# One encoder layer with product-key experts: alternating sum banks, later exponentials, eight diagonals, and an earlier load of the first merged rows

## The reference, cut to what matters

```python
h = rmsnorm(x)                        # per row
z = h @ w_in                          # attention, convolution, memory queries, gates
merged = g0 * attention(z) + g1 * conformer_conv(z) + g2 * memory_attention(z)
x = x + merged @ w_out
h = rmsnorm(x)
q = (h @ w_q).reshape(rows, 8, 2, 128)              # 8 heads, two halves each
s1, s2 = q[:, :, 0] @ keys1.T, q[:, :, 1] @ keys2.T # 128 side scores each
v1, i1 = top_k(s1, 16);  v2, i2 = top_k(s2, 16)
top, pos = top_k(v1[:, None] + v2[None, :], 16)     # 16 of 256 sums
idx = (i1 * 128 + i2)[pos]                          # one of 16384 experts
g = softmax(top)
act = gelu((h * u[idx]).sum(-1))                    # a row of u for each expert
x = x + (g * act * v[idx]).sum(experts)             # a row of v for each expert
```

## Time and profile before

| what | us |
|---|---|
| median of 3 runs | 3762.02 (3761.2 to 3765.11) |
| the profiled execution | 3731.85 |
| its span in the trace | 3730.0 |
| TensorE (PE) busy | 3340.5 (90%) |
| VectorE busy | 2929.1 (79%) |
| GpSimd busy | 2148.8 (58%) |
| ScalarE busy | 1418.8 (38%) |
| the chain that ended last: PE, VectorE, DMA, issue, POOL | 50%, 13%, 9%, 5%, 5% |

### The profile page before, as it was taken

The page is one execution under the profiler, slowest core; times in us unless marked ns, Lnnn a source line. Parts: engine busy times, 40 slices in busy tenths (PEclk is TensorE's granted clock), DMA queues, the critical chain, the costliest instruction groups (busy, mean ns, idle before and its releaser), DMA issues.

```text
span 3730.0 us, 44666 instructions
## 1 busy us (share of the span) xinstructions
PE 3340.5 (90%) x13326; PEld 2204.9 (59%) x13326; DVE 2929.1 (79%) x6686; ACT 1418.8 (38%) x2932; POOL 2148.8 (58%) x1831
## 2 busy tenths in 40 slices
PE   8999899899999949898799999999977898888966
PEld 7787555444444436666688887888844364453722
DVE  5499763467988958999988898888877878788865
ACT  5235674122442213333344444545433142332510
POOL 6221233155556545777766666676655666575776
PEclk9999999999999979999899999999988998999999
DMA  6415565698999979999999999999999999898999
GB/s 211 126 48 141 139 175 191 210 357 318 347 390 367 339 283 372 360 383 372 407 410 397 410 394 411 381 408 400 392 403 409 355 326 410 286 400 329 317 390 369
DMA packets 443310, 1224.37 MB, mean 328 GB/s; under 512 B 65250, under 2 KB 153478, under 8 KB 442047
## 3 DMA queue, kind: packets, MB, share of 16 engines
q0 software_dynamic: 239616, 872.52, 61.0%
q1 hardware_dynamic: 177162, 313.45, 24.1%
q10 hardware_dynamic: 26293, 35.54, 2.8%
HBM read 1129.03 MB, written 92.31 MB: 327 GB/s over the span
## 4 chain that ended last, share of the span: by engine, by line
PE 50%; DVE 13%; DMA 9%; issue 5%; POOL 5%; ACT 1%; SPq 0%; ACTq 0%; DVEq 0%; POOLq 0%
PE open_q_and_scores_ps L2807 18%; PE open_sums_ps L1916 8%; PE open_q_and_scores_ps L2864 4%; PE open_sums_ps L2890 4%; PE open_h_T_ps L1930 4%; DVE late_x L3290 4%; PE open_h_T_ps L2785 3%; DMA late_v_rows<-in_peer_v,table_twin_idx 3%; POOL late_v_rows L2666 2%; POOL late_u_rows L2666 2%; DVE late_u_rows L3267 2%; PE open_h_T_ps L2791 2%; PE open_h_T_ps L2717 1%; PE open_sums_ps L1856 1%; DMA open_weight_columns<-in_w_in 1%
## 5 line engine op out<-in xcount | busy, mean ns | idle before, releaser
L2666 POOL DMA_INDIRECT late_v_rows<-in_peer_v,late_kept_idx x573 | 584.4, 1020 | 210.0 <-issue 161.2
L2653 POOL DMA_INDIRECT late_u_rows<-in_peer_u,late_kept_idx x320 | 478.7, 1496 | 265.1 <-DVE late_dots L3267 205.3
L3267 DVE CUSTOM_DVE_ANT_0 late_u_rows<-late_u_rows,open_rows_ps 128x1024 f32<-128x1024 f32 x432 | 522.4, 1211 | 13.0 <-DMA late_u_rows<-in_peer_u,late_expert_idx 9.1
L3290 DVE SCALAR_TENSOR_TENSOR late_x<-late_v_rows,late_weights,late_x 128x1024 f32<-128x1024 f32 x368 | 471.5, 1281 | 10.0 <-DMA late_v_rows<-in_peer_v,late_expert_idx 6.7
L2807 PE MATMUL open_q_and_scores_ps<-table_h_T_upper,table_u_T_upper 128*128 128x512 f32 x1024 | 424.4, 414 | 0.0
L2807 PE MATMUL open_q_and_scores_ps<-table_h_T_lower,table_u_T_upper 128*128 128x512 f32 x1024 | 402.7, 393 | 0.0
L2807 PE MATMUL open_q_and_scores_ps<-table_h_T_upper,table_u_T_lower 128*128 128x512 f32 x1024 | 402.2, 393 | 0.0
L2890 PE MATMUL open_sums_ps<-late_v_rows,late_diag 128*128 128x512 f32 (+1 forms) x600 | 299.8, 636 | 85.3 <-DMA late_v_rows<-in_peer_v,late_kept_idx 34.3
L2666 POOL DMA_INDIRECT late_u_rows<-in_peer_v,late_kept_idx x259 | 284.1, 1097 | 147.2 <-issue 66.3
L2890 PE MATMUL open_sums_ps<-late_u_rows,late_diag 128*128 128x512 f32 x512 | 266.0, 660 | 84.5 <-DMA late_u_rows<-in_peer_v,late_kept_idx 43.2
L1829 POOL DMA_INDIRECT open_u_rows<-in_peer_u,late_expert_idx x115 | 161.0, 1400 | 256.5 <-DVE late_dots L2269 130.8
(11 more groups left out here) (466 smaller groups left out, 7599.2 us busy)
## 6 DMA issues: line engine op xcount, KB each, us to landing
table_u_block<-in_peer_u SPq DMA_DIRECT2D x128, 512.0 KB, 7.7
scr_scores<-table_scores SPq DMA_DIRECT2D x32, 1024.0 KB, 16.6
open_weight_columns<-in_w_in SPq DMA_DIRECT2D x64, 256.0 KB, 5.9
table_first_scores<-scr_scores SPq DMA_DIRECT2D x4, 4096.0 KB, 16.1
table_second_scores<-scr_scores SPq DMA_DIRECT2D x4, 4096.0 KB, 15.6
front_w_raw<-in_w_in SPq DMA_DIRECT2D x48, 256.0 KB, 5.0
scr_m<-open_gated SPq DMA_DIRECT2D x42, 256.0 KB, 6.1
late_v_rows<-in_peer_v,late_kept_idx POOLq DMA_INDIRECT x573, 8.8
```

The lines of the kernel that those rows point to most:

```text
L2653: pool.indirect_dma_start(u[k % U_RING][:], None, io["peer_u"][0], bass.IndirectOffsetOnAxis(ap=rows_of(n), axis=0)).then_inc(s_u[k % U_RI ...
L2666: pool.indirect_dma_start(slot[:], None, io["peer_v"][0], bass.IndirectOffsetOnAxis(ap=rows_of(m), axis=0)).then_inc(arrived, 16)
L3267: dve.tensor_tensor_reduce(u[k % U_RING][:], u[k % U_RING][:], h2_rows, 1.0, 0.0, ALU.mult, ALU.add, dots[:, n % COLS:n % COLS + 1]).then_ ...
L3290: dve.scalar_tensor_tensor(rows[:], slot[:], weight_of(m), rows[:], ALU.mult, ALU.add).then_inc(s_vsum, 1)
```

## The change

1. *Diagonals.* There are eight buffers instead of four; the four new ones lie in the table's part of SBUF.
2. *Exponentials and gates.* `exps` stands three steps behind piece 10, `gate` three steps behind piece 15 (`EXP_LAG`).
3. *Banks.* Tiles 4 and 6 sum in another pair of banks, `pRows`, tiles 3, 5 and 7 in `acc`. `keep_sum` and its semaphore are gone; `total` reads the banks. The first sum of tile 4 waits for the last dot product, that of a later tile t for `total` of tile t-2.
4. *First merged rows.* SyncE loads them behind `late_w_q_high` and ahead of the last two pairs of gated stores, into `late_h2_next` (which is in the place of a u buffer), once all units' products are done; the load after the last stores is gone. `turn_merged(1)` reads there, `normed(1)` waits until it has read, and the load of the h rows into `late_h2_next` waits for the same turn.
5. *Heads of tile 1.* The first four heads after that, R = 8 to 11, are heads 4 to 7 of the tile, which use `late_w_q_high`, and R = 12 to 15 are heads 0 to 3, so that `late_w_q_low` is waited for at R = 12 instead of 8.
6. *Residual of tile 1* stands two steps later on VectorE, as do its `square` and `normed`.

```diff
@@ -1328,3 +1328,4 @@
 COLS = 32
-DIAGS = 4
+DIAGS = 8
+EXP_LAG = 3
 HEADS_AHEAD, HEADS_KEPT = 4, 16
@@ -1348,2 +1349,4 @@
 GATE_AT = (0, 2, 1)
+HEAD_AT = [R - R % NH + (R + NH // 2) % NH if R // NH == 1 else R for R in range(HEADS)]
+HALF_FIRST = (FIRST_KEPT, NH + NH // 2)
 ROUTE, SCORES_READ = 23, 6
@@ -1497,2 +1500,3 @@
         self.row, self.ident = sb("row", [P, NK]), sb("identity", [P, P], BF16)
+        self.diag = [sb(f"diag{k}", [P, P]) for k in range(DIAGS // 2)]
         self.less_lane, self.one = sb("less_lane", [P, 1]), sb("one", [P, 1])
@@ -1765,2 +1769,9 @@
             load_chunk(j)
+        def load_first_merged(sp):
+            last = next(u for u in reversed(range(UNITS_OPEN)) if unit(u)[1] == 2)
+            sp.wait_ge(s_uprod, S0 + 2 * UNITS_OPEN)
+            for g in (2 * last, 2 * last + 1):
+                sp.wait_ge(s_mst[g % GATED_RING], S0 + 16 * (g // GATED_RING + 1))
+            sp.dma_start(L.h2_next[:], scr["m"][1]).then_inc(L.s_m, 16)
+
         for u in range(UNITS_OPEN):
@@ -1789,2 +1800,4 @@
                 load_conv(u + CONV_RING)
+            if u + 1 == UNITS_OPEN:
+                load_first_merged(sp)
             for h in range(2):
@@ -2416,3 +2429,3 @@
     ss, root, inv, twins, B = L.ss, L.root, L.inv, L.twins, L.table
-    dots, gl, wt, diag, qs, qT, u, v, tile_sum = L.dots, L.gl, L.wt, L.diag, L.qs, L.qT, L.u, L.v, L.tile_sum
+    dots, gl, wt, diag, qs, qT, u, v, tile_sum = L.dots, L.gl, L.wt, L.diag + L.table.diag, L.qs, L.qT, L.u, L.v, L.tile_sum
     top, topi, topf, hot = L.top, L.topi, L.topf, L.hot
@@ -2432,3 +2445,3 @@
     s_sq, s_root, s_inv = p.sem("x2_squares"), p.sem("x2_root"), p.sem("x2_scale")
-    s_x2, s_y, s_yout, s_tile = (p.sem(n) for n in ("x2_summed", "y_rows", "y_stored", "tile_sum"))
+    s_x2, s_y, s_yout = (p.sem(n) for n in ("x2_summed", "y_rows", "y_stored"))
     s_q, s_qk, s_qt, s_qtk, s_sc = (p.sem(n) for n in ("q", "q_kept", "q_turned", "qT_kept", "side_scores"))
@@ -2455,2 +2468,6 @@
 
+    def banks_of(t):
+
+        return pRows if t in TABLED[::2] else acc
+
     def two_back(R):
@@ -2512,8 +2529,4 @@
         def load_merged(t):
-            if t >= 2:
-                sp.wait_ge(s_hturn, S0 + t)
-                sp.wait_ge(s_h2out.sem, s_h2out.start + 16 * min(t - 1, SHORT))
-            else:
-                sp.wait_ge(s_hturn, S0 + 1)
-                sp.wait_ge(s_place, S0 + 1)
+            sp.wait_ge(s_hturn, S0 + t)
+            sp.wait_ge(s_h2out.sem, s_h2out.start + 16 * min(t - 1, SHORT))
             sp.dma_start(h2[:], scr["m"][NE if t == SHORT else prompt_tile(t)]).then_inc(s_m, 16)
@@ -2556,2 +2569,4 @@
                 sp.wait_ge(s_place, S0 + t)
+            else:
+                sp.wait_ge(s_mturn, S0 + 2)
             sp.dma_start(h2_next[:], scr["h2"][t]).then_inc(s_h2in.sem, 16)
@@ -2594,3 +2609,2 @@
 
-        load_merged(1)
         load_x_new(1)
@@ -2706,3 +2720,3 @@
             for k in range(KC):
-                src = h2[:, k * P:(k + 1) * P] if t else done.gated[k // 4][:, k % 4 * P:(k % 4 + 1) * P]
+                src = (h2_next if t == 1 else h2)[:, k * P:(k + 1) * P] if t else done.gated[k // 4][:, k % 4 * P:(k % 4 + 1) * P]
                 ins = pe.transpose(chain_banks(t)[:, k // 4, (k % 4) * P:(k % 4 + 1) * P], src, c.ident[:])
@@ -2731,5 +2745,6 @@
             else:
-                if R in (4, 8):
-                    L.w_q[R % NH // 4].wait(pe)
-                columns = L.w_q[R % NH // 4].buf[:, :, R % 4 * 2 * NK:(R % 4 + 1) * 2 * NK]
+                H = HEAD_AT[R]
+                if R in HALF_FIRST:
+                    L.w_q[H % NH // 4].wait(pe)
+                columns = L.w_q[H % NH // 4].buf[:, :, H % 4 * 2 * NK:(H % 4 + 1) * 2 * NK]
             pe.wait_ge(s_hT, S0 + R // NH + 1)
@@ -2753,3 +2768,3 @@
             for s in range(2):
-                ins = pe.matmul(pS[:, 0, s * NK:(s + 1) * NK], qT[:, s, :], keysT[:, 2 * (R % NH) + s, :], start=True, stop=True)
+                ins = pe.matmul(pS[:, 0, s * NK:(s + 1) * NK], qT[:, s, :], keysT[:, 2 * (HEAD_AT[R] % NH) + s, :], start=True, stop=True)
             ins.then_inc(s_sc, 1)
@@ -2879,5 +2894,5 @@
                 elif t == FIRST_TABLED:
-                    pe.wait_ge(s_y, S0 + 1)
-                elif t > FIRST_TABLED:
-                    pe.wait_ge(s_tile, S0 + t - FIRST_TABLED)
+                    pe.wait_ge(s_dot, S0 + DOTS[GATHER_END])
+                else:
+                    pe.wait_ge(s_y, S0 + t - FIRST_TABLED)
             if m == last_of(SHORT):
@@ -2889,3 +2904,3 @@
             for h in range(2):
-                ins = pe.matmul(acc[0:rows, h, :], diag[k % DIAGS][:, 0:rows], slot[:, h * BANK:(h + 1) * BANK],
+                ins = pe.matmul(banks_of(t)[0:rows, h, :], diag[k % DIAGS][:, 0:rows], slot[:, h * BANK:(h + 1) * BANK],
                                 start=(m == first_of(t)), stop=(m == last_of(t)), skip_group_check=True)
@@ -2957,7 +2972,7 @@
             act.wait_ge(s_sck.sem, s_sck.start + i + 1)
-            act.dma_start(scr["side"][R], L.side_stage[i % 2][:]).then_inc(s_scout[i % 2].sem, 16)
+            act.dma_start(scr["side"][HEAD_AT[R]], L.side_stage[i % 2][:]).then_inc(s_scout[i % 2].sem, 16)
 
         def load_side(R):
-            i = R - FIRST_KEPT
-            act.wait_ge(s_scout[i % 2].sem, s_scout[i % 2].start + 16 * (i // 2 + 1))
+            i, at = R - FIRST_KEPT, HEAD_AT.index(R) - FIRST_KEPT
+            act.wait_ge(s_scout[at % 2].sem, s_scout[at % 2].start + 16 * (at // 2 + 1))
             if i == 0:
@@ -2985,3 +3000,3 @@
                         keep_merged(t + 1)
-                    if t < NE and h == (2 if t == 0 else 6):
+                    if t < NE and h == (3 if t == 0 else 6):
                         square(t + 1)
@@ -3075,7 +3090,2 @@
 
-        def keep_sum(t):
-            act.wait_ge(s_sum, S0 + TENSOR_SUMS[tile_end(t)])
-            act.wait_ge(s_y, S0 + t - SHORT)
-            act.activation(tile_sum[:], acc[:].rearrange("p a n -> p (a n)"), ACT.Copy).then_inc(s_tile, 1)
-
         ahead = Names()
@@ -3107,8 +3117,5 @@
                 diagonal(m)
-            for R, piece in ROUTES_AT.get(n, ()):
+            for R, piece in ROUTES_AT.get(n - EXP_LAG, ()):
                 if piece == 10:
                     exps(R)
-            for t in TABLED[:-1]:
-                if n == tile_end(t) + TENSOR_LAG:
-                    keep_sum(t)
 
@@ -3237,2 +3244,4 @@
             dve.reciprocal(inv[:], root[:]).then_inc(s_inv, 1)
+            if t == 1:
+                dve.wait_ge(s_hturn, S0 + 1)
             dve.wait_ge(s_inv, S0 + t + 1)
@@ -3254,9 +3263,6 @@
             rows = SAM if t == SHORT else P
-            if t in (SHORT, NE):
-                dve.wait_ge(s_sum, S0 + TENSOR_SUMS[tile_end(t)])
-            else:
-                dve.wait_ge(s_tile, S0 + t - SHORT)
+            dve.wait_ge(s_sum, S0 + TENSOR_SUMS[tile_end(t)])
             dve.wait_ge(s_vsum, S0 + VECTOR_SUMS[tile_end(t)])
             dve.wait_ge(s_x2in[t % 2].sem, s_x2in[t % 2].start + 16 * ((t + 1) // 2))
-            rows_sum = acc[0:rows, :, :].rearrange("p a n -> p (a n)") if t in (SHORT, NE) else tile_sum[:]
+            rows_sum = banks_of(t)[0:rows, :, :].rearrange("p a n -> p (a n)")
             dve.tensor_tensor(summed(t)[0:rows, :], rows_sum, summed(t)[0:rows, :], ALU.add).then_inc(s_y, 1)
@@ -3307,5 +3313,5 @@
                 for h in range(NH - FIRST_KEPT if t == 0 else NH):
-                    if t < NE and h == (1 if t == 0 else 5):
+                    if t < NE and h == (2 if t == 0 else 5):
                         residual(t + 1)
-                    elif t < NE and h == (2 if t == 0 else 6):
+                    elif t < NE and h == (3 if t == 0 else 6):
                         normed(t + 1)
@@ -3365,3 +3371,3 @@
                 gate(2)
-            for R, piece in ROUTES_AT.get(n - 1, ()):
+            for R, piece in ROUTES_AT.get(n - EXP_LAG, ()):
                 if piece == TOPK - 1:
```

2 lines of the change are left out of this document (1 added, 1 removed).

## The result

The changed kernel takes 3734.94 us (median of 4 runs, 3730.49 to 3739.79), the kernel before 3761.61 (3759.85 to 3765.11, 4 runs). The ratio is 0.9928, with a 95% interval of 0.9911 to 0.9945: 26.7 us faster. The forecast was 3730, -32.

The account below looks back on a forecast made before the run. No engine bounds throughout: VectorE, then TensorE in the table stage and picks, DMA share 0.93 or more in those windows. Terms -19 and -13 sum to -32 us, from 3762 to 3730, range 3713 to 3754.

Parts of the forecast that it names:

- The front term: Early merged rows and tile 1's residual two steps later: tile 0's last sum ends 19.0 us earlier, kept to the end.
- the two steps: VectorE steps following tile 1's residual, 7.4 us, were to run inside VectorE's wait for that residual.
- The late term: Exponentials three steps later and eight diagonals: held back sums run before keys are complete, 13 us, bounds 0 and 15.9.
- The gaps: TensorE between last keys and `turn_keys`, tiles 5 to 7: 4.75, 6.15 and 4.99 us, to fall under 2.
- The parts at 0: Tile 1's reordered heads, priced 0, and banks instead of copies, 0 with bounds 0 and 3.1 us.
- The waits of the earlier trace: Late stage, TensorE for diagonals 52.5 us and ScalarE before exponentials 92.7; both were to become less.
- the idle stretch in front of tile 2's residual: On VectorE; as long as that before tile 1's residual, 26.43 us, it would show the forecast wrong.
- Only the front term: Transfers set the pick stage's start, earlier keys meet later rows: -19 us only, median 3743; chance 0.20.
- The clock: TensorE idles before the picks and begins them at low clock: 8.6 us lost over three tiles, median 3739; chance 0.07.
- Nothing that can be told: The 19 us are given back before 1812 as DMA saturates, and the late stage gains 0; chance 0.10.
- Slower: Late exponentials make VectorE wait before rewriting `late_best`, 24 heads x 1.8 us = 43 us, median 3786; chance 0.08.
- The distance of 30 us: Median of the runs, 3762.02, stood 30.2 us above the profiled execution, 3731.85; the forecast kept that distance.

Follow-up runs that it names:

- the front part alone: Kernel before with merged rows loaded early, tile 1's heads reordered and its residual two steps later: ratio 0.9944, -21 us.
- the load alone: Kernel before with only the earlier load of the first merged rows, residual and heads in the old order: ratio 0.9962, -14 us.
- second profile of before: Kernel before, unchanged, run once more with a profile: 3738.58 us; without the profiler median 3733.7 us.
- the late part: Kernel before with eight diagonals, exponentials and gates three steps later, and alternating banks without a copy: ratio 0.9984, -6 us.
- the exponentials alone: Kernel before with exponentials and gates three steps later for all heads, four diagonals, one pair of banks, copies: ratio 0.9982, -7 us.
- the second profile of the changed kernel: Changed kernel, no edit, run once more with a profile: 3708.40 us, ratio 0.9924.
- the five steps: Changed kernel with exponentials and gates five steps later instead of three, for tiles 5 to 7 only: ratio 0.9937 to the kernel before.

## Why the prediction was right

**The front term** was forecast at -19 us and is -21 in the time (interval -14 to -28) and -20.5 in the trace of the front part alone. Its steps hold. From the opening's end tile 1's turn comes 11.7 us earlier (forecast 11.6), its residual 13.9 (11.6), as it follows the turn 2.3 us sooner, and the end of the last sum 21.4 (19.0), as the two steps bring 7.5 (7.4). The residual of tile 2 comes 19.9 and 17.2 us earlier in the two profiles of the changed kernel (19.0). That the last sum's clock time agrees to 0.1 us (1355.94, 1355.8) is chance: the later end of the opening hides the difference. Divided by landmarks: at the last sum the load alone gives 11.8 us (11.6 forecast) and the shift 9.3 (7.4); the order of heads gives 0 or a small loss (0).

One step went wrong and was made good by luck. `normed` was to follow the residual as before; it waits 8.85 us for the root of ScalarE, which is behind the queries' copies, so h is stored at 1366.37, 5.5 us later than 1379.90 - 19.0 = 1360.9. But that store took 19.62 us instead of the 24.89 that the prediction kept, and tile 2's rows were turned 18.9 us earlier all the same. The store now starts 10.4 us behind the issue of `late_w_q_low` instead of 5.1; that this makes it shorter is likely, but no run shows it.

**The late term** was forecast at -13, and here a term was mis-sized. The gaps went as forecast: 4.94, 4.98 and 4.68 us in the second profile of before became 0.62, 0.06 and 0.63 in that of the changed kernel, 13.3 less. Of that 7 to 11 us come out in the distance from tile 4's to tile 7's keys, comparing traces with the same front, in five traces (708.0 and 705.1 against 715.3 and 716.3; 704.4, 705.2 and 702.5 against 712.6), and nothing in the first profile of the changed kernel (714.4), for a reason that isn't known. Some 3 us of the rest are TensorE's lower clock behind the keys (below). Where the exponentials are late in the tiles 5 to 7 only, the time agrees with the forecast: 0.9911 against the front part's 0.9944 is -12 us, from two occasions.

What was missing in the sum is the table stage. The step "in the table stage the 112.3 us that VectorE waits for exponentials are worth nothing" looked at VectorE alone and priced the move of the exponentials of the heads up to 39 on ScalarE at 0. VectorE's wait grew to 132.8 us, and that is indeed worth nothing, but TensorE, the bound there, waits where exponentials and a gelu meet between two copies: at seven places instead of five, at three of them 1.43 to 1.47 us instead of at one. TensorE's waits for ScalarE rise from 2.7 to 5.7 us and its busy time in the stage from 884.0 to 886.1; in all the stage takes 4.9 to 6.2 us more. With that the late part is -6 us in the time (interval -11 to -1), and -7 (-11 to -3) with the exponentials alone.

So the total of -26.7 us lies as near to -32 as it does also because the two misses have opposite signs: 2 us more in front, 7 less behind.

**The parts at 0.** Banks and diagonals were priced at nothing and as help for the exponentials. They are worth nothing that can be told (0.9995, 0.9996), and the help isn't needed either.

**The signs.** Most of those that the prediction named came. Two did not. The waits of the earlier trace rows did not become less, as told above. And the idle stretch in front of tile 2's residual, named as a sign of being wrong, came in part (15.61 and 19.05 us). It is no loss: where the gates stand as before, VectorE waits at a gate instead (15.19 us), and the residual comes no earlier.

**The rivals.** *Only the front term* comes within 8 us of the result (3743), for the wrong reason: the late gain is there, part of it is lost in the table stage, not to the transfers. *The clock* is there, at about a third of its price (3 us for the three tiles instead of 8.6). The granted clock in the 10 us behind the turn of tile 6's keys, before and in the second profile of the changed kernel:

```profile
3217.69:3227.69 10.00, 10.00 (x44) 6.52 (x43) 1.45 (x11) 5.33 (x10) 5.58 (x6) 1.00 0.91 321
...
3200.83:3210.83 10.00, 10.00 (x40) 6.51 (x41) 3.84 (x12) 5.15 (x10) 7.59 (x8) 0.92 0.89 304
```

At tiles 5 and 7 it is 1.00 before and 0.90 and 0.91 after. TensorE idles 3.6 us ahead of each tile's last sum (3.64 in the first fence of tile 6 above), and that sum, the transposes and the next sum are slow: 0.29 to 0.32, 0.63 and 2.51 to 2.65 us behind the keys instead of 0.22, 0.39 and 1.94, or 0.9 to 1.1 us a tile instead of the 2.9 of the rival. The last sum itself takes 3.78 us instead of 1.88 at tiles 5 and 7, which is why a gap of 0.6 us stays there; at tile 6 it ends before the keys are written and costs nothing. The rule of the Trainium skill that the prediction cites ("TensorE: Matmul & The Clock Gate", Part 1: The HAM clock gate) holds in so far: the sums behind an idle stretch are slow, and the one at 3210.34 takes the full rate's 1.88 us again. But the same idle time does not always do it: with the exponentials late in tiles 5 to 7 only, TensorE idles 3.58 us ahead of tile 6's last sum, which then takes 1.98 us, and the clock behind the turn is 1.00. *Nothing that can be told* fell with both parts. *Slower* fell too, and the five steps show why its price was off.

**The distance of 30 us** between the profiled execution and the median was kept as it was, and rightly for a median measured on the same occasion. Why runs of the earlier occasion take 27 us more than the later ones, of either kernel, stays open; the chip may be another, as the record has none for the first runs.

## What to carry to other kernels

Where one engine waits behind a transfer, look at what the issuing queue did first: here the data were ready and the issue stood behind other stores, and the time of the transfers was lost at a place behind which they were saturated (a share of 0.23, then 0.93 to 1.02). When an instruction is moved on an engine, price it in every stage in which it is issued, by what then stands next to it there, and not by the engine that waits for it. And test the supporting parts of a change alone: eight diagonals and the second pair of banks can be left out, within what these runs can tell.

The best version measured is the front part with exponentials late in the tiles 5 to 7 only (0.9910). Leaving out the new order of heads as well, which the experiments suggest, wasn't tried.

## What the runs showed of the hardware

A load of ScalarE's function table takes 1.28 us in the trace, and the next instruction starts 0.01 us behind it. Two loads between two copies that TensorE waits for cost it 1.43 to 1.47 us of waiting and its block of the table 1.7 us at the worst places, and 0.3 and 0.6 us at the others, depending on where between the copies they fall; the pattern was the same in every trace of a kernel with the same order. A stage bound by TensorE repeated to 0.8 us in 891 over ten traces, while the last column of the table, where TensorE and VectorE wait 60 to 71 us each for gathered rows, varied by 16 us. After 3.6 us of idle time four 128x512 matmuls took 2.59 to 3.78 us in the changed kernel's second profile, and 1.98 in another kernel's.
